# Seven-product form for the second block's values and late tile pairs, with work moved to GpSimd and ScalarE

## The chip, the cores and the metric

The kernel runs on one core of a Trainium2 chip. The metric is the device time of one execution in microseconds (us). Engines are named as the profile names them: PE is TensorE, PEld its weight loads, DVE VectorE, ACT ScalarE, POOL GpSimd, SP SyncE (which only issues DMAs here). All data is float32; TensorE runs one float32 matrix product as two records in the trace, so a count of records is twice the count of `matmul` calls.

## The reference, cut to what matters

The program is two blocks of a language model. The change is in the second block, which runs twice (DEPTH = 2) on 256 tokens of width 1024:

```python
def token_mixer(x, w_in, ...):
    m = x @ w_in                                   # 1024 -> 3*1024 + 2*1024 + 2*1024 columns
    q, k, v, xr, gr, gates = jnp.split(m, cuts, axis=-1)
    ya = diff_attention(q, k, v, lambda_qk, subln_g, lam_init)   # 8 heads, softmax twice per head
    h = rg_lru(causal_conv(xr, conv_w, conv_b), ...)             # 4 taps along the tokens
    yr = h * jax.nn.gelu(gr)
    g = jax.nn.sigmoid(gates.reshape(B, S, N_BRANCH, D_MODEL))
    merged = g[:, :, 0] * (ya @ w_br_attn) + g[:, :, 1] * (yr @ w_br_lru)
    return merged @ w_out

def causal_conv(xb, w, b):
    y = b + xp[:, 0:S] * w[0]
    for tap in range(1, CONV_W):
        y = y + xp[:, tap:tap + S] * w[tap]
```

Behind the mixer come a layer norm, a mixture of experts picked by key (`peer`) and a second layer norm.

## The kernel before, in words

The kernel is a chain of phases. Within a phase each engine has its own list of instructions in a fixed, hand-written order, and waits on semaphores; between phases all engines meet, so a phase ends when its last engine is done. Three phases in a row matter here, once in each of the two layers.

**Queries and keys, then values** (L2255 to L2452). `m = x @ w_in` is computed transposed, in tiles of 128 output columns by 256 tokens. Two such tiles (a tile pair, one 1 MB weight DMA) are one 2x2 block product, and eight pairs make the queries and keys. They are already in seven-product form (Strassen's scheme as Winograd arranged it): instead of eight products of half-size blocks, seven, with sums of weight blocks and of token blocks as operands. Each product is four calls of `product()` (L2296) of 128x128 by 128 columns, 28 calls for a pair. VectorE makes the four weight sums (`weight_sum`, L2353, 128x512 each) one pair ahead, and adds the partial results out of PSUM; ScalarE copies two parts. The seventh product, `onto` a PSUM bank, has to wait until VectorE has read that bank (semaphore `third`). The values follow as plain products: 32 calls of 128x128 by 512 columns (L2335), each of four PSUM banks copied out by VectorE (L2450).

**Attention with the late tile pairs** (L2454 to L2619). Attention is done in eight units (two heads by 128 query tokens). Units 0 to 3 see 128 keys ("early" here), units 4 to 7 see 256 ("late"). For each unit TensorE forms scores (L2503), VectorE adds the position bias and takes the maximum (L2559), ScalarE takes exponentials (L2602), VectorE sums them, scales and subtracts the two softmaxes (L2564 to L2571), TensorE turns the result (L2516) and multiplies it by the values (L2529), VectorE copies that out (L2578). The remaining 16 tile pairs of `x @ w_in`, the late pairs, are put between these steps on TensorE, two for each unit, as plain products: 16 calls of 128x128 by 256 columns for a pair (L2478), each result copied out of PSUM by one ScalarE instruction (L2588). VectorE does the convolution, one column tile in four instructions (L2547, L2549), in units 2 to 5. GpSimd does nothing. The last late product is split, and its second half is put behind the sums of squares over each head (`head_sums`, L253), whose root (L2616) and reciprocal (L2582) end the phase.

**Gates and branches** (from L2622), unchanged, begin with L2693 and L261 on TensorE; L261 reads the reciprocal.

SP's list of weight DMAs: `w.rest` alternates two buffers, so a load starts when the pair two before it is done.

Of the kernel before, what the change touches and what calls it, by code (L numbers as in the profile page):

```python
# [12 lines left out]
ALU = mybir.AluOpType  # L13
# [3 lines left out]
P = 128  # L17
D = 1024
# [2160 lines left out]
def second_block(nc, a, w, h, scaled, spare, cst, psum, psum_all):  # L2179

    with ExitStack() as ctx:
# [37 lines left out]
        for l in range(DEPTH):  # L2219
            tile = {n: (lambda i, n=n: a[n][l, i]) for n in ("w_in2", "br_attn", "br_lru", "w_out2", "peer_q")}  # L2220
            with ExitStack() as mixer:
# [14 lines left out]
                with ExitStack():  # L2236
# [8 lines left out]
                    part = arena[:, beside:beside + 4 * 2 * HALF].rearrange("p (q b t) -> p q b t", q=4, b=2)  # L2245
                    P1, P5, U2, U3 = range(4)
# [5 lines left out]
                    with phase(nc, "extra", "products", "weight_sums", "input_sums", "copied", "second", "third", "fourth", "taken", "scaled_out", "vectors", "v_weights", "v_ready", "soft_exp", "soft_log", "lam_sums", "lam_exp",  # L2252
                               "constants", "root", "h_ready", shared=w.landed[0]) as (block, S):
                        @block.sync
                        def _(sp):  # L2255
# [5 lines left out]
                            w.first(sp, 1, late_tile, W2)  # L2261

                        @block.scalar
                        def _(act):
# [3 lines left out]
                            for p in range(QK):  # L2268
# [8 lines left out]
                                if p % 2 == 0:  # L2277
                                    act.dma_start(wv[:, p:p + 2, :], a["w_v2"][l][:, p:p + 2, :]).then_inc(S.v_weights, 16)
# [9 lines left out]
                            act.activation(lam[:, 2:4], lam[:, 0:2], ACT.Exp).then_inc(S.lam_exp, 1)  # L2288
                            act.wait_ge(S.constants, 16)

                        @block.tensor
                        def _(pe):
# [35 lines left out]
                            pe.wait_ge(S.taken, 3 * QK)  # L2328
                            pe.wait_ge(S.v_weights, 16 * KD // 2)
                            if l == 0:  # L2330
                                pe.wait_ge(S.h_ready, KD)
                            for n in range(QT):
                                for half in range(2):
# [3 lines left out]
                                    mm.then_inc(S.v_ready, 1)  # L2337

                        @block.vector
                        def _(dve):  # L2340
# [13 lines left out]

                            def input_sum(n):
# [3 lines left out]
                                one, two = ((x_in[:, :, 0, hi], x_in[:, :, 0, lo]), (x_in[:, :, 1, hi], tin[:, 0]),  # L2359
# [35 lines left out]
                            for n in range(4):  # L2395
                                weight_sum(0, n)
                                input_sum(n)
# [1111 lines left out]
```

## Time and profile before

| | us |
|---|---|
| median of 3 runs (3458.3 to 3463.97) | 3458.74 |
| profiled execution | 3461.76 |
| its span | 3460.0 |
| PE busy in the span | 3157.5 |
| DVE busy | 2265.3 |
| ACT busy | 724.6 |
| POOL busy | 602.4 |
| queries and keys, layer 0, PE starts | 1493.5 |
| values, layer 0, PE starts | 1546.74 |
| attention phase, layer 0, PE starts | 1575.74 |
| next phase, layer 0, PE starts | 1707.58 |
| the same attention phase in layer 1, to the next phase | 2688.20 |

How to read it: PE is busy 91% of the span, and in the phases above nearly all the time; busy counts overlapping records once. The phases are read from a timeline, in which a row is a run of like instructions on one engine. "idle before" in brackets says how long the engine had nothing to do ahead of the row, and what ended that. Layer 1 repeats layer 0 within a few tenths of a microsecond, so every price below is read in layer 0 and counted twice.

### The profile page before, as it was taken

To read this page: it belongs to the slowest core of one execution; us is meant where nothing else is said; L and a number is where in the kernel's file an instruction comes from. 1 tells how busy PE (TensorE), PEld (TensorE's weight loads), DVE (VectorE), ACT (ScalarE), POOL (GpSimd) and SP (SyncE) were. 2 spreads that over 40 slices of the span, in tenths; PEclk is the share of its full clock that TensorE was granted. 3 is DMA by queue.
4 is the path that set the end of the run, shared out by engine and by line. 5 is a ranking of instruction groups with operands and counts; after the bars stand their busy time and mean duration, and the time that the engine had idled before them with its cause. 6 is when DMAs were issued, how large, how long until landed. Compare 5 with 4: busy or idle time off the path is not lost. (4 is left out here: it accounts for less than half of the span.)

```text
span 3460.0 us, 55458 instructions
## 1 busy us (share of the span) xinstructions
PE 3157.5 (91%) x20794; PEld 2381.9 (69%) x20794; DVE 2265.3 (65%) x5751; ACT 724.6 (21%) x1787; POOL 602.4 (17%) x520
## 2 busy tenths in 40 slices
PE   8999889999899999999998888888899989888877
PEld 8996679999878979987885444333678864434433
DVE  8844658778675558763458777776634567777775
ACT  2101311111131211111412222222212322222222
POOL 0000100000000000000004544445000035444442
PEclk9999899999999999999999999999999999999999
DMA  5443024444312024452449999999734479999998
GB/s 203 162 161 121 1 86 159 162 176 176 125 71 77 4 79 167 170 198 98 158 189 394 421 422 422 422 422 421 297 113 158 195 293 421 421 422 422 422 421 332
DMA packets 116014, 829.18 MB, mean 240 GB/s; under 512 B 12784, under 2 KB 14320, under 8 KB 17424
## 3 DMA queue, kind: packets, MB, share of 16 engines
q0 software_dynamic: 73728, 536.90, 37.4%
q1 hardware_dynamic: 39488, 273.59, 21.1%
q10 hardware_dynamic: 2576, 15.59, 1.3%
q8 instruction: 155, 2.54, 0.3%
q14 instruction: 67, 0.55, 0.0%
HBM read 824.99 MB, written 1.05 MB: 239 GB/s over the span
## 5 line engine op out<-in xcount | busy, mean ns | idle before, releaser
L3215 PE MATMUL psum_all<-expert_rows,const_sb 128*128 128x512 f32 x2048 | 971.3, 632 | 181.0 <-ACT const_sb L3130 180.1
L2803 POOL DMA_INDIRECT expert_rows<-in_peer_uv_dram,head_experts x512 | 593.1, 1158 | 2426.8 <-issue 1864.8
L3215 PEld LDWEIGHTS psum_all<-expert_rows,const_sb 128*128 128x128 f32 x2048 | 403.9, 202 | 730.6 <-issue 472.8
L2955 DVE CUSTOM_DVE_ANT_0 expert_rows<-expert_rows,xn 128x1024 f32<-128x1024 f32 x512 | 616.5, 1223 | 255.6 <-DMA expert_rows<-in_peer_uv_dram,head_experts 251.6
L2478 PE MATMUL psum_all<-x,weight_ring 128*128 128x256 f32 x1024 | 228.6, 381 | 0.0
L3130 ACT ACTIVATE const_sb<-cst,head_weights 128x128 f32<-128x128 f32 x496 | 158.6, 390 | 329.2 <-DVE head_weights L2966 318.4
L2478 PEld LDWEIGHTS psum_all<-x,weight_ring 128*128 128x128 f32 x1024 | 191.7, 190 | 28.8 <-issue 3.5
L409 PE MATMUL psum_all<-xn,weight_ring 128*128 128x136 f32 (+1 forms) x1408 | 193.0, 280 | 20.2 <-PEq L174 9.1
L409 PEld LDWEIGHTS psum_all<-xn,weight_ring 128*128 128x128 f32 x1408 | 176.6, 192 | 21.7 <-issue 9.8
L409 PE MATMUL psum_all<-xn,weight_sums 128*128 128x136 f32 (+1 forms) x1056 | 142.6, 278 | 0.7 <-DVEq L641 0.6
L3126 ACT ACTIVATE dots<-dots 128x4 f32<-128x4 f32 x124 | 25.5, 205 | 559.7 <-DVE dots L2955 559.7
L409 PE MATMUL psum_all<-input_sums,weight_sums 128*128 128x136 f32 (+1 forms) x1056 | 132.6, 278 | 0.1
L409 PEld LDWEIGHTS psum_all<-xn,weight_sums 128*128 128x128 f32 x1056 | 130.9, 191 | 1.2 <-issue 1.2
L409 PEld LDWEIGHTS psum_all<-input_sums,weight_sums 128*128 128x128 f32 x1056 | 126.8, 191 | 0.6 <-issue 0.4
L518 ACT ACTIVATE gate<-gate 128x272 f32<-128x272 f32 (+1 forms) x88 | 37.5, 426 | 361.2 <-DVE gate L611 361.2
L571 DVE TENSOR_TENSOR weight_sums<-weight_ring 128x512 f32<-128x512 f32 (+1 forms) x102 | 68.4, 671 | 58.7 <-PE psum_all L409 55.6
L409 PE MATMUL psum_all<-hidden,weight_ring 128*128 128x136 f32 (+1 forms) x704 | 88.7, 278 | 0.0
L3197 PE MATMUL psum_all<-x,weight_ring 128*128 128x256 f32 x384 | 84.8, 379 | 0.0
L409 PEld LDWEIGHTS psum_all<-hidden,weight_ring 128*128 128x128 f32 x704 | 84.4, 190 | 0.0
L3197 PEld LDWEIGHTS psum_all<-x,weight_ring 128*128 128x128 f32 x384 | 73.0, 190 | 15.0 <-issue 5.7
L2578 DVE COPY expert_rows<-psum_all 128x256 f32<-128x256 f32 x16 | 6.8, 424 | 114.5 <-PE psum_all L2529 114.5
L280 PE MATMUL psum_all<-xn,weight_ring 128*128 128x272 f32 x320 | 75.2, 398 | 0.0
(621 smaller groups left out, 5082.1 us busy)
## 6 DMA issues: line engine op xcount, KB each, us to landing
weight_ring<-in_ffn_in_dram SPq DMA_DIRECT2D x88, 1024.0 KB, 4.8
weight_ring<-in_w_in_dram SPq DMA_DIRECT2D x48, 1024.0 KB, 4.8
weight_ring<-in_ffn_out_dram SPq DMA_DIRECT2D x32, 1024.0 KB, 4.8
weight_ring<-in_ffn_out_dram SPq DMA_DIRECT2D x16, 768.0 KB, 4.2
weight_ring<-in_hyb_in_dram SPq DMA_DIRECT2D x12, 1024.0 KB, 4.8
weight_ring<-in_peer_q_dram SPq DMA_DIRECT2D x12, 1024.0 KB
expert_rows<-in_w_v_dram ACTq DMA_DIRECT2D x8, 1024.0 KB, 5.7
weight_ring<-in_br_attn_dram SPq DMA_DIRECT2D x8, 1024.0 KB, 6.8
```

What stands on the lines that cost most here:

```text
L280: mm = pe.matmul(banks[s * halves + h], wt[:, h, k, :], rhs[:, k, :], start=(k == 0), stop=(k == ktiles - 1))
L409: mm = pe.matmul(out, left(j), right(j), start=first and j == js[0], stop=end and j == js[-1], skip_group_check=onto)
L518: act.activation(gate[:, p % 2, :], gate[:, p % 2, :], ACT.Silu).then_inc(S.gate_ready, 1)
L571: dve.tensor_tensor(ws[:, 0], wt[:, 1, :, 0, :], wt[:, 1, :, 1, :], ALU.add).then_inc(S.weight_sums, 1)
L2478: mm = pe.matmul(late_bank(t)[:, half * T2:(half + 1) * T2], wt[:, half, k, :], h[:, k, :], start=(k == 0), stop=(k == KD - 1))
L2578: dve.tensor_copy(oa[:, 2 * hp:2 * hp + 2, n * P:(n + 1) * P], psum[5][:, 0:2 * P].rearrange("p (j t) -> p j t", j=2)).then_inc(S.attn_rea ...
L2803: pool.indirect_dma_start(out=rows[:, j, :], out_offset=None, in_=a["peer_uv"], in_offset=bass.IndirectOffsetOnAxis(ap=idx[:, n, j:j + 1], ...
L2955: dve.tensor_tensor_reduce(row, row, xt[:, n, :], 1.0, 0.0, ALU.mult, ALU.add, dots[:, n, j:j + 1]).then_inc(S.dotted, 1)
L3126: act.activation(dots[:, n, at], dots[:, n, at], ACT.Gelu_apprx_tanh).then_inc(S.gelus, 1)
L3130: act.activation(diag[:, j, :], ident, ACT.Copy, scale=wts[:, n, j:j + 1]).then_inc(S.diagonals, 1)
L3197: mm = pe.matmul(query_bank[:, c, :], wt[:, c, k, :], h[:, k, :], start=(k == 0), stop=(k == KD - 1))
L3215: mm = pe.matmul(sums(n, half), diag[:, j, :], rows[:, j, D + half * 512:D + (half + 1) * 512], start=False, stop=last and j == TOPK - 1)
```

## The change

1. The values take the seven-product form too: 7 products of 4 calls of 128x128 by 512 columns (28 calls in place of 32). VectorE makes their weight sums (`v_sum`, eight instructions of 128x1024) and, in layer 0, new token sums (`v_input`), in the last pair of the keys and beside the values' own products. Their weights are requested in the first four tile pairs instead of every second one.
2. The 16 late pairs take the seven-product form with 128 columns: 28 calls of `product()` in place of 16 with 256 columns. They use one set of four PSUM banks; the scores now have one buffer in place of two.
3. The four weight sums of each late pair are made by GpSimd (128x512 each), those of the first two pairs already at the end of the values' phase. They wait until the pair two before has been multiplied.
4. Results of a late pair leave PSUM by three ScalarE copies and four VectorE additions, with a fifth addition between two SBUF tiles, all 128x128.
5. The convolution leaves VectorE: ScalarE forms four products of 128x256 for a column tile (`conv_products`), after the pairs named in `CONV_AFTER`, and GpSimd adds three of them (`add_tap`), two additions after each pair's sums from pair 5 on.
6. Scores of the next unit are added on VectorE, and their exponentials taken on ScalarE, within the present unit.
7. Weight loads of the late pairs use three buffers.

In the rows of order below, `psum_all` is PSUM, `weight_ring` the raw weights as they land, `expert_rows` the big SBUF tile that holds everything else of this phase, `x` the tokens. TensorE in the fifth unit (unit 4, 256 keys) stood so before:

```order
L2503 MATMUL psum_all<-expert_rows 128x256 x4
L2478 MATMUL psum_all<-x,weight_ring 128x256 x16
L2516 MATMUL psum_all<-cst,expert_rows 128x128 x4
L2478 MATMUL psum_all<-x,weight_ring 128x256 x16
L2529 MATMUL psum_all<-expert_rows 128x128 x4
```

The same place of the changed kernel, as far as the transposes (L2692):

```order
L2675 MATMUL psum_all<-expert_rows 128x256 x4
L2623 MATMUL psum_all<-x,weight_ring 128x128 x4
L2623 MATMUL psum_all<-expert_rows 128x128 x12
L2623 MATMUL psum_all<-x,weight_ring 128x128 x4
L2623 MATMUL psum_all<-x,expert_rows 128x128 x4
L2623 MATMUL psum_all<-expert_rows,weight_ring 128x128 x4
L2692 MATMUL psum_all<-cst,expert_rows 128x128 x4
```

The 16 calls have become seven products of four; the last of them is the seventh product, which waits for `third`. A second pair of the same rows follows the transposes.

VectorE in that unit stood so before, from the copy of the unit ahead (L2578) on, the convolution at its end:

```order
L2578 COPY expert_rows<-psum_all 128x2x128
L2559 ISA expert_rows<-psum_all,const_sb 128x256
L2562 TENSOR_SCALAR expert_rows<-expert_rows 128x4
L2564 TENSOR_REDUCE expert_rows<-expert_rows 128x4
L2565 RECIPROCAL expert_rows<-expert_rows 128x4
L2566 TENSOR_SCALAR expert_rows<-expert_rows,lam 128x2
L2568 TENSOR_SCALAR expert_rows<-expert_rows 128x256 x2
L2571 SCALAR_TENSOR_TENSOR expert_rows<-expert_rows 128x256 x2
L2547 TENSOR_SCALAR expert_rows<-expert_rows,vec_sb 128x256
L2549 SCALAR_TENSOR_TENSOR expert_rows<-expert_rows,vec_sb 128x256 x3
```

and stands so in the changed kernel, where L2721 and L2724 are the two additions that release `second` and `third`:

```order
L2772 COPY expert_rows<-psum_all 128x2x128
L2757 TENSOR_REDUCE expert_rows<-expert_rows 128x4
L2758 RECIPROCAL expert_rows<-expert_rows 128x4
L2759 TENSOR_SCALAR expert_rows<-expert_rows,lam 128x2
L2761 TENSOR_SCALAR expert_rows<-expert_rows 128x256 x2
L2764 SCALAR_TENSOR_TENSOR expert_rows<-expert_rows 128x256 x2
L2721 TENSOR_TENSOR expert_rows<-expert_rows,psum_all 128x128
L2724 TENSOR_TENSOR expert_rows<-expert_rows,psum_all 128x128
L2747 ISA expert_rows<-psum_all,const_sb 128x256
L2750 TENSOR_SCALAR expert_rows<-expert_rows 128x4
L2731 TENSOR_TENSOR expert_rows<-expert_rows,psum_all 128x128
L2734 TENSOR_TENSOR expert_rows<-expert_rows 128x128
```

The softmax of the unit now stands directly ahead of `third`, and the bias and maximum of the next unit (L2747, L2750) behind it.

At the end of the phase TensorE had eight calls of the last late pair behind `head_sums` (L253):

```order
L2529 MATMUL psum_all<-expert_rows 128x128 x4
L2478 MATMUL psum_all<-x,weight_ring 128x256 x4
L253 MATMUL psum_all<-expert_rows,cst 8x256 x8
L2478 MATMUL psum_all<-x,weight_ring 128x256 x8
```

and has four half as wide now:

```order
L2704 MATMUL psum_all<-expert_rows 128x128 x4
L2623 MATMUL psum_all<-x,weight_ring 128x128 x4
L2623 MATMUL psum_all<-x,expert_rows 128x128 x4
L253 MATMUL psum_all<-expert_rows,cst 8x256 x8
L2623 MATMUL psum_all<-expert_rows,weight_ring 128x128 x4
```

The diff, cut to its core:

```diff
+ v_product(v_bank[0], lambda j: h_pairs[:, j, 0, lo], lambda j: v_raw[:, j, 0, :, 0, :])
+ pe.wait_ge(S.v_sums, 2)
+ v_product(v_bank[1], lambda j: tin[:, 0, j, :], lambda j: v_sums[:, 0, j])
...
+ pe.wait_ge(S.v_third, 1)
+ v_product(v_bank[3], lambda j: tin[:, 3, j, :], lambda j: v_raw[:, j, 1, :, 1, :], onto=True)
- for k in range(KD):
-     mm = pe.matmul(psum[4 + 2 * n + half][:, :], h[:, k, n * P:(n + 1) * P], wv[:, k, half * 512:(half + 1) * 512],
-                    start=(k == 0), stop=(k == KD - 1))
+ @block.gpsimd                       # phase of the values
+     pool.wait_ge(S.products, PRODUCTS * QK)
+     pool.wait_ge(S.v_products, 4)
+     pool.wait_ge(S.v_sums, 8)
+     for t in range(2):              # the four weight sums of late pairs 0 and 1
...
+ @block.gpsimd                       # phase of the attention
+     def add_tap(n):
+         k = n // 3
+         pool.wait_ge(S.tap_products, n + k + 2)
+         if n % 3:
+             pool.wait_ge(S.taps_added, n)
+         pool.tensor_tensor(xc[:, k, :], xc[:, k, :], tap_product(n), ALU.add).then_inc(S.taps_added, 1)
+     for t in range(EARLY_SUMS, LATE):
+         pool.wait_ge(*late_landed(S, t))
+         pool.wait_ge(S.products, PRODUCTS * (t - 1))
+         pool.tensor_tensor(ws[:, 0], wt[:, 1, :, 0, :], wt[:, 1, :, 1, :], ALU.add).then_inc(S.weight_sums, 1)
+         pool.wait_ge(S.weight_sums, done + 1)
+         pool.tensor_tensor(ws[:, 1], ws[:, 0], wt[:, 0, :, 0, :], ALU.subtract).then_inc(S.weight_sums, 1)
+         pool.tensor_tensor(ws[:, 2], wt[:, 0, :, 0, :], wt[:, 1, :, 0, :], ALU.subtract).then_inc(S.weight_sums, 1)
+         pool.wait_ge(S.weight_sums, done + 2)
+         pool.tensor_tensor(ws[:, 3], wt[:, 0, :, 1, :], ws[:, 1], ALU.subtract).then_inc(S.weight_sums, 1)
+         if t >= 5:
+             add_tap(2 * t - 10)
+             add_tap(2 * t - 9)
+ CONV_AFTER = {2: 0, 4: 1, 5: 2, 7: 3, 8: 4, 10: 5, 11: 6, 13: 7}
  @block.tensor
  for u, (hp, n) in enumerate(units):
-     if u + 1 < len(units):
+     if 0 < u and u + 1 < len(units):
          score(u + 1)
-     late_product(per_unit * u)
+     late_begin(2 * u)               # products 1 to 4
+     late_onto(2 * u)                # 5 and 6: wait for ScalarE's two copies
+     late_end(2 * u)                 # 7: waits for third
      pe.wait_ge(S.probs, u + 1)
...
+ @block.vector
+     for u in range(len(units)):
+         if u:
+             late_take(2 * u - 1)
+             take_out(u - 1)
+         weigh(u)
+         late_parts(2 * u)           # second, third
+         if u + 1 < len(units):
+             add(u + 1)
+         late_take(2 * u)
+         late_parts(2 * u + 1)
+ @block.scalar
+     for u, (hp, n) in enumerate(units):
+         copy_parts(2 * u)
+         if u:
+             head_squares(u - 1)
+         take_low(2 * u)
+         if u + 1 < len(units):
+             exps(u + 1)
+         conv_products(2 * u)
+         act.wait_ge(S.turned, u + 1)
...
+         copy_parts(2 * u + 1)
```

## Rows read from the trace of the kernel before

**Rows 1.** Windows, keys and attention: us, then PE, PEld, DVE, ACT, POOL busy, clock.
```profile
1493.00:1546.70 53.70, 52.25 (x449) 51.73 (x448) 43.29 (x101) 10.46 (x24) 0.00 (x0) 0.97 0.67 249
1575.70:1707.50 131.80, 130.66 (x664) 111.39 (x664) 51.37 (x170) 28.86 (x66) 0.00 (x0) 1.00 0.38 136
```

**Rows 2.** Groups: the late products in the attention phase; busy, mean ns, idle.
```profile
L2478 PE MATMUL psum_all<-x,weight_ring 128*128 128x256 f32 x512 | 114.3, 381 | 0.0
```

**Rows 3.** Timeline: last key pair, then the values; start, length, engine, line.
```profile
1540.73 2.76 PEld L2296 LDWEIGHTS psum_all<-expert_rows 128*128 128x128 f32 x24
1543.41 0.97 PEld L2296 LDWEIGHTS psum_all<-xn,weight_ring 128*128 128x128 f32 x8
1546.74 27.73 PE L2335 MATMUL psum_all<-expert_rows,x 128*128 128x512 f32 x64 [0.38 <-DVE expert_rows L2386]
```

**Rows 4.** Timeline of PE: unit 1 begins, unit 2 begins, then unit 4 to unit 5.
```profile
1591.58 0.72 PE L2503 MATMUL psum_all<-expert_rows 64*128 64x128 f32 x8
...
1606.91 0.72 PE L2503 MATMUL psum_all<-expert_rows 64*128 64x128 f32 x8
...
1654.40 1.14 PE L2503 MATMUL psum_all<-expert_rows 64*128 64x256 f32 x8
...
1655.47 7.17 PE L2478 MATMUL psum_all<-x,weight_ring 128*128 128x256 f32 x32
...
1669.83 1.05 PE L2529 MATMUL psum_all<-expert_rows 128*128 128x128 f32 x8
...
1670.81 1.14 PE L2503 MATMUL psum_all<-expert_rows 64*128 64x256 f32 x8
```

**Rows 5.** Timeline of DVE and ACT within a unit of 256 keys.
```profile
1656.97 1.71 ACT L2602 ACTIVATE expert_rows<-expert_rows 128x256 f32<-128x256 f32 x4 [2.76 <-DVE expert_rows L2562]
1658.71 1.22 DVE L2564 TENSOR_REDUCE expert_rows<-expert_rows 128x4 f32<-128x1024 f32 x1 [1.77 <-ACT expert_rows L2602]
...
1661.10 0.88 DVE L2571 SCALAR_TENSOR_TENSOR expert_rows<-expert_rows 128x256 f32<-128x256 f32 x2
...
1670.99 0.42 DVE L2578 COPY expert_rows<-psum_all 128x256 f32<-128x256 f32 x1 [5.11 <-PE psum_all L2529]
```

**Rows 6.** Timeline in the first block: all places where POOL computes beside DVE.
```profile
384.12 2.89 POOL L1211 TENSOR_TENSOR qd<-gq,eg 128x1280 f32<-128x1280 f32 x1 [48.92 <-ACT eg L1251]
384.25 0.42 DVE L1130 CUSTOM_DVE_ANT_0 fox_s<-psum_all,weight_ring 16x272 f32<-16x272 f32 x1
...
385.07 1.96 DVE L1134 TENSOR_SCALAR fox_stat<-fox_stat 16x2 f32<-16x2 f32 x1
...
389.28 0.71 DVE L1194 TENSOR_TENSOR fox_s<-fox_s,fox_stat 16x544 f32<-16x544 f32 x1
...
392.81 2.89 POOL L1215 TENSOR_TENSOR kbg<-kb,eg 128x1280 f32<-128x1280 f32 x1
...
393.60 2.68 DVE L1194 TENSOR_TENSOR fox_s<-fox_s,fox_stat 16x544 f32<-16x544 f32 x1
```

**Rows 7.** Timeline: end of the attention phase and first product of the next.
```profile
1699.36 3.62 PE L253 MATMUL psum_all<-expert_rows,cst 128*8 128x256 f32 x16
...
1702.91 3.72 PE L2478 MATMUL psum_all<-x,weight_ring 128*128 128x256 f32 x16
1703.02 0.37 ACT L2616 ACTIVATE rs<-psum_all 8x256 f32<-8x256 f32 x1 [3.10 <-PE psum_all L253]
1703.49 1.74 DVE L2582 RECIPROCAL rs<-rs 8x256 f32<-8x256 f32 x1 [5.26 <-ACT rs L2616]
...
1707.58 1.97 PE L2693 MATMUL psum_all<-expert_rows 128*128 128x256 f32 x8 [0.94 <-PEq L174]
```

**Rows 8.** Groups: the instructions whose like are added; busy, mean ns, idle.
```profile
L2353 DVE TENSOR_TENSOR expert_rows<-weight_ring 128x512 f32<-128x512 f32 x16 | 11.0, 685 | 2.1 <-PEq L174 2.1
L2367 DVE TENSOR_TENSOR expert_rows<-expert_rows,psum_all 128x128 f32<-128x128 f32 x8 | 2.3, 282 | 2.0 <-PE psum_all L2296 2.0
L2594 ACT ACTIVATE expert_rows<-expert_rows 128x256 f32<-128x256 f32 x8 | 3.2, 403 | 2.5 <-DVE expert_rows L2578 2.5
```

More of the change, by code:

```diff
@@ L2251, in second_block @@
                     quad = lambda p: [psum[4 * (p % 2) + i][:, 0:HALF] for i in range(4)]
-                    with phase(nc, "extra", "products", "weight_sums", "input_sums", "copied", "second", "third", "fourth", "taken", "scaled_out", "vectors", "v_weights", "v_ready", "soft_exp", "soft_log", "lam_sums", "lam_exp",
-                               "constants", "root", "h_ready", shared=w.landed[0]) as (block, S):
+                    QUARTER = D // 4
+                    v_sums = arena[:, NQK * (PADC + T2):NQK * (PADC + T2) + 4 * KP * 2 * QUARTER].rearrange("p (s j g m) -> p s j g m", s=4, j=KP, g=2)
@@ L2327, in _, with v_product @@
                                 product(bank[3], lambda j: wt[:, 1, j, 1, :], lambda j: tin[:, 3, j, :], onto=True)
-                            pe.wait_ge(S.taken, 3 * QK)
-                            pe.wait_ge(S.v_weights, 16 * KD // 2)
+                            def v_product(out, left, right, onto=False):
+                                for j in range(KP):
+                                    mm = pe.matmul(out, left(j), right(j), start=j == 0 and not onto, stop=j == KP - 1, skip_group_check=onto)
+                                mm.then_inc(S.v_products, 1)
@@ L2459, in second_block @@
                     pt = area(work + 8 * T2, 2, QT, P)
[L2460 to L2466 removed]
+                    st = area(work + 8 * T2 + 2 * QT * P, 2, 4, 4)
@@ new lines, in second_block @@
+                    late_quad = [psum[b][:, 0:HALF] for b in (6, 7, 2, 3)]
+                    late_out = lambda t: (z[:, NQK + 2 * t, PADC:], z[:, NQK + 2 * t + 1, PADC:])
+                    with phase(nc, "extra", "products", "weight_sums", "copied", "second", "third", "fourth", "taken", "low_taken", "scores", "added", "shifted", "exps", "probs",
+                               "turned", "turned_in", "attn_out", "attn_read", "o_squares", "o_sums", "o_root", "tap_products", "taps_added", shared=w.landed[1]) as (block, S):
@@ L2552, in _, with late_parts @@
-                            for u, (hp, n) in enumerate(units):
+                            def late_parts(t):
+                                bank, b = late_quad, t % 2
+                                dve.wait_ge(S.products, PRODUCTS * t + 3)
+                                dve.wait_ge(S.copied, 2 * t + 1)
+                                dve.tensor_tensor(part[:, U2, b, :], part[:, P1, b, :], bank[2], ALU.add).then_inc(S.second, 1)
+                                dve.wait_ge(S.products, PRODUCTS * t + 4)
+                                dve.wait_ge(S.second, t + 1)
+                                dve.tensor_tensor(part[:, U3, b, :], part[:, U2, b, :], bank[3], ALU.add).then_inc(S.third, 1)
@@ L2553, in _, with add @@
+                            def add(u):
+                                hp, n = units[u]
                                 kn = (n + 1) * P
@@ L2590, in head_squares, with exps @@
+                            def exps(u):
+                                act.wait_ge(S.shifted, u + 1)
+                                for c in range(4):
+                                    s = s_sb[:, u % 2, c, 0:(units[u][1] + 1) * P]
+                                    last = act.activation(s, s, ACT.Exp, bias=st[:, u % 2, 3, c:c + 1], scale=AD ** -0.5)
+                                last.then_inc(S.exps, 1)
                             def head_squares(u):
```

300 lines of the change are left out of this document (224 added, 76 removed).

## The prediction

> **What bounds the kernel now.** I read the page first (PE busy 91%), then the windows of the three phases, then the timeline of single units. In the keys PE is busy 52.25 of 53.70 us, in the attention phase 130.66 of 131.80, while DVE works 51.37, ACT 28.86 and POOL not at all [rows 1]. So TensorE's own work is the length of these phases, and a product taken away is worth its full time, as long as nothing that feeds TensorE comes late. The reader is to see in the timeline of PE that its rows follow each other without a gap [rows 4].
>
> **What the change takes away.** A late pair costs 114.3 / 16 = 7.14 us [rows 2]. In the seven-product form a pair is 56 records; 24 of them take 1543.41 - 1540.73 = 2.68 us in the keys, which run this form now, so 0.112 us each and 6.25 us a pair [rows 3]. Gain 0.89 x 16 = 14.2 us a layer. The values are 27.73 us for 32 calls; 28 of the same shape are 24.3, gain 3.5 us, and the 0.38 us that PE waits ahead of them goes too, since the new banks are free sooner [rows 3]. Against it, VectorE has four value sums twice as long as a weight sum (0.685 us, [rows 8]) ahead of the last key pair's additions: that pair's seventh product comes about 0.3 us late. Values: 3.5 a layer. The other value sums and token sums end on VectorE about 7 us after the keys, under products 1 and 2 (3.5 us each) or later; product 6 needs the last sums, which are made during product 4. The eight early GpSimd sums start at the end of product 4, and three products, 10.4 us, stand beside them; at 1.2 us each (below) they end at 10, just inside. Request times of the weights move by a few us in queues with room; I cost that at nothing. If nothing waited, two layers would give 2 x (14.2 + 3.5) = 35.4 us.
>
> **What it adds, and where it lies on the path.** GpSimd: a 128x1280 addition-like instruction takes 2.89 us [rows 6]; in proportion 128x512 takes 1.16. The trace has no such row. Below I bound it by this 1.16; above by 2.89 itself, since a fixed part can't be excluded from one size. I take 1.2, near the proportional end, which is where the one row points. A pair's four sums are then 5.1 us with the steps between, two additions of the convolution 1.4: 6.5 against 7 to 8 us for a pair and its share of attention. GpSimd keeps up, and has 6 us of lead before TensorE would wait for a sum.
>
> But GpSimd holds VectorE up. While POOL computes from 384.12 to 387.01, a DVE TENSOR_SCALAR of 16x2 lasts 1.96 us and ends at 387.03; the second L1194, begun at 393.60, takes 2.68 us where the first took 0.71, and ends 0.58 after POOL does at 395.70. The CUSTOM instruction that reads PSUM and one SBUF tile, in between, takes its usual 0.42 [rows 6]. I carry that over: in the attention phase every TENSOR_SCALAR and every instruction with two SBUF inputs waits for the running POOL instruction; reductions and additions out of PSUM don't. The Trainium skill, "SBUF — State Buffer", Who interferes with whom, says the same more sharply: one port pair is shared, held for a whole instruction, and the second to issue blocks fully; the trace agrees in its three overlaps. By that rule alone the sum is the one made here.
>
> Now one late unit, time 0 where the unit's scores begin. TensorE: scores 1.07 [rows 4], six products of 0.89, so the seventh could start at 6.4. VectorE: sees the end of the product with the values at 0.2, copies 0.4, the chain from reduction to subtraction 3.27 (1658.71 to 1661.98, [rows 5]), two additions of 0.28 [rows 8] with 0.2 between and behind: `third` at 4.6. Spare: 1.8 us. GpSimd starts its sums when the pair ahead ends, 1 us before 0 (1669.83 to 1670.81, [rows 4]), so it runs 1.2 us instructions from -0.9 to 4.2 and convolution additions to 5.7. In the 3.27 us chain the first TENSOR_SCALAR comes at 2.0 and waits to 2.95 (0.9); the scaling pair behind it finds the next POOL instruction begun, 1.1; the subtraction pair finds an addition of the convolution, 0.55. Together 2.55, less the spare 1.8: the seventh product waits 0.8 us. Of a pair of like instructions I let only the first wait; if each does, 0.6 more. In an early unit the chain is shorter by 0.8 and the scores by 0.5, and the same three waits leave 0.7. The last unit has no scores ahead of it, so 0.8 + 1.07 = 1.85. Over the eight units: 0.2 + 0.7 + 0.75 + 0.2 + 3 x 0.8 + 1.85 = 6.1 us a layer (in unit 3 the scores are already long and the chain still short).
>
> Behind `third` stands the next unit's bias and maximum, then its small TENSOR_SCALAR at 8.7, again behind a POOL instruction (begun at 8.2): 9.4. ScalarE waits for it, then exponentials 1.71 to 11.3 [rows 5], and, after pairs 2, 4, 8 and 10, four products of the convolution at 0.4 [rows 8] to 13.0; then the copy of the turned result 0.6 and of the first part of the odd pair 0.3: 13.9. TensorE has the odd pair's first four products done at 12.1 and stands until 14.0: 1.9 us in units 4 and 5. Without convolution ScalarE is in time, but VectorE frees the bank of the odd pair's second product about 0.5 late (units 3 and 6, together 1.15); early units 0.15 twice. Sum 5.25 us a layer.
>
> The end: `head_sums` runs 1699.36 to 1702.91, then 3.55 us of products cover root and reciprocal (to 1705.23) [rows 7]. Now 0.89 covers them. DVE's last addition waits for that product and ends 1.4 after `head_sums`, the reciprocal 1.74 later, the meeting of engines 0.3: next phase at 3.5 to 3.7 in place of 4.67. Of the 2.7 that TensorE saves here 1.7 isn't had.
>
> **Sum.** A layer: 14.2 - 6.1 - 5.25 - 1.7 + 3.5 = 4.7; two layers 9.4 us. The profiled execution took 3461.76, the span 3460.0; 3461.76 - 9.4 = 3452.4. The median of the runs shown is 3.0 lower, so 3449.
>
> **Rivals.** (a) *The waits are light.* If VectorE's held instructions slip between POOL's, or an own start falls past a boundary, 1.3 us of waits in place of 2.55 stays within the spare 1.8. Left are the end, 1.7, and about 1.5 a layer for ScalarE and the last unit: gain 2 x (14.2 + 3.5 - 3.2) = 29, time 3430. For it: the waits sit just above a threshold. Against: sums and chain both start from TensorE's steps, so their order is the same in each unit. (b) *Each held instruction waits*, 0.6 more in six units, 3.6 a layer: 9.4 - 7.2 = 2.2, time 3456.5. (c) *Slower: GpSimd's 128x512 costs more than proportion.* Each 0.1 us adds 0.3 in seven chains and 0.1 in the stretch behind, 2.8 a layer, 5.6 in all. No gain is left at 1.2 + 0.17 = 1.37 us; at 1.6 us four sums and two additions take 8.4 us, more than a pair, TensorE also waits for sums, and the loss is 22 - 9 = 13 or more: 3472. From 1.48 us on it is slower by over 7 us. A fixed part of 0.5 us in each POOL instruction would do; at the upper bound, 2.89, 56 sums alone need 162 us in a phase of 118, and the time would be near 3550. The Trainium skill, "GPSIMD Engine Reference", Elementwise — side-by-side cycle accounting, gives 4497 ns for 2048 columns; with the 2.89 us row a line through both would give 1.3 us, an estimate, and by it 3455. (d) *The change does as it says without any hold*: 35.4 less the end 3.4 and 1 of ScalarE, 31: 3428. The low end.
>
> **How the numbers follow.** Forecast as walked, 3443 to 3453, 0.42. Light waits or none (a, d), 3428 to 3443: 0.27. More waits (b, or c up to 1.45 us), 3453 to 3465: 0.19. Slower (c beyond): 0.12. About 0.2%, 7 us, is what can be told from no change. Faster (below 3451.8): 0.27 and 0.34 of the 0.42, together 0.61. Same: the other 0.08 and 0.19, together 0.27. Slower: 0.12. The range takes the low end of (d) and stops a little below the slow case: 3429 to 3464.
>
> **What would show it.** The values' 56 records in 24.3 us; a late pair on PE 6.25 where nothing waits; POOL TENSOR_TENSOR of 128x512 at 1.2 us; in the chain of each unit, DVE TENSOR_SCALAR and SCALAR_TENSOR_TENSOR of 1 us or more that end with a POOL instruction; PE idle 0.7 to 0.9 us ahead of the seventh product of even pairs, released by the VectorE addition L2724; 1.9 us in units 4 and 5, released by ScalarE's copy; the next phase 3.6 us behind `head_sums`. Wrong if the held instructions keep their old length, if POOL's means lie above 1.4 us, or if PE waits for weight sums.

## The result and the profile after

| | before | after |
|---|---|---|
| median, us | 3462.29 (3458.3 to 3466.28, 11 runs) | 3467.48 (3462.78 to 3475.72, 11 runs) |
| ratio, 95% interval | | 1.0022 [1.0014, 1.003] |
| span of the profiled execution | 3460.0 | 3464.1 |

The change makes the kernel slower by about 0.2%. The prediction said 3449 in a range of 3429 to 3464: wrong in sign and outside the range.

Starts of the phases on TensorE give the length of each phase, in us:

| | before, layer 0 / 1 | after, layer 0 / 1 |
|---|---|---|
| queries and keys | 53.25 / 53.43 | 52.23 / 53.05 |
| values | 29.00 / 29.00 | 25.54 / 25.53 |
| attention with late pairs | 131.84 / 131.82 | 134.48 / 134.46 |
| gates, up to the first branch product | 11.21 / 11.22 | 19.47 / 19.47 |
| from there to the next layer's keys, or to the end | 755.2 / 760.6 | 750.3 / 756.8 |

Windows of the kernel after, the phases of layer 0 and last the gates of layer 1; columns as in [rows 1] (us, then PE, PEld, DVE, ACT, POOL busy, granted clock):

```profile
1492.76:1544.99 52.23, 51.46 (x448) 51.10 (x449) 46.41 (x101) 9.97 (x24) 0.00 (x0) 0.98 0.69 252
1544.99:1570.53 25.54, 24.21 (x59) 10.49 (x57) 15.02 (x37) 2.23 (x5) 10.25 (x8) 1.00 0.08 33
1570.53:1705.01 134.48, 123.55 (x1049) 115.99 (x1049) 86.11 (x218) 44.48 (x131) 87.78 (x80) 1.00 0.38 134
1705.01:1724.48 19.47, 19.47 (x49) 13.93 (x50) 5.83 (x11) 10.02 (x22) 0.00 (x0) 0.56 0.41 162
2687.82:2707.29 19.47, 19.47 (x49) 13.90 (x50) 5.83 (x11) 10.06 (x22) 0.00 (x0) 0.56 0.42 162
```

The window of the gates in the kernel before:

```profile
1707.58:1718.79 11.21, 11.21 (x48) 8.79 (x49) 5.53 (x11) 8.84 (x21) 0.00 (x0) 1.00 0.71 283
```

Two things are to be seen. In the attention phase PE is busy 7.1 us less than in [rows 1], but idle 10.9 us in place of 1.1. And in the gates, whose instructions the change doesn't touch, the same work takes 8.26 us more: PE is busy all the time, and its granted clock is 0.56 in place of 1.00.

PE's timeline at that place, which answers to [rows 7] (start, length, line, records, idle before):

```profile
1697.60 3.62 PE L253 MATMUL psum_all<-expert_rows,cst 128*8 128x256 f32 x16
1701.15 1.16 PE L2623 MATMUL psum_all<-expert_rows,weight_ring 128*128 128x128 f32 x8
...
1705.01 2.64 PE L2939 MATMUL psum_all<-expert_rows 128*128 128x256 f32 x8 [2.70 <-PEq L174]
1707.58 3.78 PE L261 MATMUL psum_all<-rs,cst 8*128 8x256 f32 x8
1711.29 3.78 PE L2939 MATMUL psum_all<-expert_rows 128*128 128x256 f32 x8
...
1718.71 5.93 PE L2939 MATMUL psum_all<-expert_rows 128*128 128x256 f32 x16
```

The idle ahead of the gates has grown from 0.94 to 2.70 us. Behind it eight records of L2939 soon take 3.78 us where they took 1.97 in [rows 7]: TensorE runs at the lower of its two levels, 1.2 GHz in place of 2.4, until late in the last row.

What PE waited for from the attention phase to the meeting behind it (who waited, for whom; us in total, times, longest):

```profile
PE psum_all L2623 <- DVE expert_rows L2724: 4.5, 5, 2.2
PE psum_all L2939 <- PEq L174: 2.7, 1, 2.7
PE psum_all L2623 <- DVE expert_rows L2731: 2.0, 4, 0.7
PE psum_all L2623 <- ACT expert_rows L2799: 1.7, 2, 0.9
```

L2724 is the addition `third`, L2731 the one that frees the bank of the second product, L2799 ScalarE's copy of the first product. The unit that the prediction walked, unit 4, from where its scores begin (1629.79):

```profile
1632.13 1.27 POOL L2607 TENSOR_TENSOR expert_rows<-weight_ring 128x512 f32<-128x512 f32 x1
1632.23 2.60 DVE L2761 TENSOR_SCALAR expert_rows<-expert_rows 128x256 f32<-128x256 f32 x2
1633.36 1.32 POOL L2609 TENSOR_TENSOR expert_rows<-weight_ring,expert_rows 128x512 f32<-128x512 f32 x1
1634.65 1.64 POOL L2597 TENSOR_TENSOR expert_rows<-expert_rows 128x256 f32<-128x256 f32 x2
1634.87 1.70 DVE L2764 SCALAR_TENSOR_TENSOR expert_rows<-expert_rows 128x256 f32<-128x256 f32 x2
1636.49 0.27 DVE L2721 TENSOR_TENSOR expert_rows<-expert_rows,psum_all 128x128 f32<-128x128 f32 x1
1636.87 0.29 DVE L2724 TENSOR_TENSOR expert_rows<-expert_rows,psum_all 128x128 f32<-128x128 f32 x1
1637.21 1.16 PE L2623 MATMUL psum_all<-expert_rows,weight_ring 128*128 128x128 f32 x8 [0.73 <-DVE expert_rows L2724]
```

The two instructions of the scaling pair L2761, asked for one by one, run from 1632.23 to 1633.55 and from 1633.48 to 1634.83: each ends 0.15 us behind a POOL instruction (1633.40 and 1634.68). The pair takes 2.60 us in place of some 0.7. `third` ends at 1637.16, and the seventh product waits 0.73 us for it.

### The profile page after: what moved, and what is told of

Its sections match the earlier page's. It is cut to its first block and busy times, and to the rows that moved or that the text cites. A ratio compares the mean times of both kernels' runs of the same rounds, so it can differ in the third digit from the quotient of the medians.

```text
span 3464.1 us, 57647 instructions
## 1 busy us (share of the span) xinstructions
PE 3133.3 (90%) x21546; PEld 2388.9 (69%) x21546; DVE 2356.7 (68%) x5869; ACT 760.7 (22%) x1921; POOL 793.0 (23%) x696
## 5 line engine op out<-in xcount | busy, mean ns | idle before, releaser
L3461 PE MATMUL psum_all<-expert_rows,const_sb 128*128 128x512 f32 x2048 | 956.0, 624 | 193.5 <-ACT const_sb L3376 193.4
L2623 PE MATMUL psum_all<-expert_rows 128*128 128x128 f32 x768 | 91.6, 276 | 4.0 <-DVE expert_rows L2731 4.0
L2623 PEld LDWEIGHTS psum_all<-expert_rows 128*128 128x128 f32 x768 | 88.3, 192 | 5.3 <-POOL expert_rows L2604 5.3
L3443 PE MATMUL psum_all<-x,weight_ring 128*128 128x256 f32 x384 | 84.8, 379 | 0.0
L3443 PEld LDWEIGHTS psum_all<-x,weight_ring 128*128 128x128 f32 x384 | 73.0, 190 | 15.0 <-issue 5.7
```

The source lines that it names most:

```text
L2623: mm = pe.matmul(out, left(j), right(j), start=j == 0 and not onto, stop=j == KP - 1, skip_group_check=onto)
L3443: mm = pe.matmul(query_bank[:, c, :], wt[:, c, k, :], h[:, k, :], start=(k == 0), stop=(k == KD - 1))
L3461: mm = pe.matmul(sums(n, half), diag[:, j, :], rows[:, j, D + half * 512:D + (half + 1) * 512], start=False, stop=last and j == TOPK - 1)
```

## Experiments

All ratios are to the kernel before, run beside each. Lengths of stretches and stops are those of the profiled execution. Edits are cut to their core, and are against the kernel after unless said otherwise. "Theory C" in some expectations is the reading above: the idle at the meeting lets TensorE's clock fall.

**1. Cover for the idle.** Five matmuls whose result nobody reads, behind the last product of the phase:

```diff
+ for j in range(5):
+     pe.matmul(banks[0], ident, h[:, j, :], start=True, stop=True)
```

> The changed kernel with five more 128x128 by 256-column products behind the attention phase's last late product, into a PSUM bank that nobody reads (2.2 us of work, in the 2.70 us that PE stands idle there). Theory C (the idle stretch lets PE's granted clock fall, and the next phase then runs at half speed for 19.5 us): the phase's length stays 134.5 us a layer, PE's granted clock in the 19.5 us behind it is 1.0 again instead of 0.56, and that stretch shrinks from 19.5 to about 11.2 us; the kernel gets 16 us faster than the changed one, about 3451, 0.3% under the kernel before. Rival (the slow stretch comes from its inputs or from other engines): stretch and time unchanged, about 3467.

Measured: 3463.77, ratio 1.0006 [0.9996, 1.0016]. Layer 0:

```profile
1690.30 1.66 PE L2623 MATMUL psum_all<-expert_rows,weight_ring 128*128 128x128 f32 x8 [2.22 <-DVE expert_rows L2726]
...
1707.13 1.96 PE L2941 MATMUL psum_all<-expert_rows 128*128 128x256 f32 x8 [0.54 <-PEq L174]
1709.02 1.99 PE L261 MATMUL psum_all<-rs,cst 8*128 8x256 f32 x8
```

With 0.54 us of idle the gates take 11.21 us in both layers, as before. The meeting is the same, at the same 3.86 us behind the sums over the heads, only filled: without the idle the gates weren't slow. The gain in time was a third of what was expected, 0.16% or some 5.5 us between the ratios of the two kernels. In layer 0 the clock now fell for a moment inside the last unit (1.66 where eight such records take 1.16), 1.7 us in the phase, and the stretch from the branches to the next layer took 755.2 us, not the 750.3 of after (761.4 and 756.8 in layer 1).

**2. GpSimd made thin.** The sums and additions of GpSimd in the attention phase on one column (so the late pairs' and convolution's values are not computed); all waits stay:

```diff
- pool.tensor_tensor(ws[:, 0], wt[:, 1, :, 0, :], wt[:, 1, :, 1, :], ALU.add)
+ pool.tensor_tensor(ws[:, 0, 0, 0:1], wt[:, 1, 0, 0, 0:1], wt[:, 1, 0, 1, 0:1], ALU.add)
```

> The changed kernel with GpSimd's weight sums and additions in the attention phase cut to one column each (the rest of them is left out), all waits kept. Theory W (VectorE's held instructions wait for running GpSimd instructions): no TENSOR_SCALAR or SCALAR_TENSOR_TENSOR of more than 0.9 us, no PE wait for the addition that releases the seventh product except 0.7 in the last unit, the phase 134.5 - 7 = about 127.5 us a layer; the slow stretch behind it stays. Time about 3467 - 14 = 3453. Rival (the units are long because of ScalarE and the order of steps, not GpSimd): phase 133 or more, time above 3463.

Measured: 3444.41, 0.9937 [0.9921, 0.9953]. The attention phase is 123.00 us in both layers, and no stop behind L2724, L2731 or L2799 is left. The groups of DVE, of after and then of this kernel (line, shape, count, busy us, mean ns):

```profile
L2761 DVE TENSOR_SCALAR expert_rows<-expert_rows 128x256 f32<-128x256 f32 x8 | 8.8, 1134 | 0.1
L2759 DVE TENSOR_SCALAR expert_rows<-expert_rows,lam 128x2 f32<-128x2 f32 x8 | 7.8, 973 | 0.3
L2764 DVE SCALAR_TENSOR_TENSOR expert_rows<-expert_rows 128x256 f32<-128x256 f32 x8 | 6.1, 803 | 0.1
```

```profile
L2764 DVE SCALAR_TENSOR_TENSOR expert_rows<-expert_rows 128x256 f32<-128x256 f32 x8 | 3.5, 482 | 0.1
L2761 DVE TENSOR_SCALAR expert_rows<-expert_rows 128x256 f32<-128x256 f32 x8 | 2.5, 351 | 0.1
L2759 DVE TENSOR_SCALAR expert_rows<-expert_rows,lam 128x2 f32<-128x2 f32 x8 | 1.8, 228 | 0.3
```

An instruction on two elements a partition takes 973 ns beside GpSimd and 228 without. The whole price of letting GpSimd's 80 instructions do their work is 134.48 - 123.00 = 11.5 us a layer. The idle at the meeting was still 2.69 us. Behind it the clock was low for some 4 us in layer 0 (gates 12.85), and for longer in layer 1 (20.72, which is 9.5 over 11.21).

**3. The values alone** (against before: only the values in seven-product form, the late pairs as they were):

> The kernel before with the values alone in seven-product form: late pairs, convolution and attention as before, nothing on GpSimd. Theory: values' phase 3.4 us shorter in each layer, attention 131.8 us and the next phase 11.2 us as before; time 7 us under the kernel before (ratio 0.998). Rival (the values' part costs elsewhere, for instance by its earlier weight requests in the keys): ratio 1.000 or more.

Measured: 3456.14, 0.9979 [0.997, 0.9988], values 25.53 us, attention phase 131.82, gates 11.22. That half of the change brings what was predicted of it.

**4. The idle alone, in the kernel before.** The whole last late product is done ahead of the sums over the heads, so nothing covers root and reciprocal:

```diff
+ late_part(last_late, 1, range(KD)).then_inc(S.late_ready, 1)
  head_sums(...)
- late_part(last_late, 1, range(KD)).then_inc(S.late_ready, 1)
```

> The kernel before, with the half late product that stands behind the sums over heads put ahead of them, so that PE has nothing while root and reciprocal are made: PE idle there 0.94 + about 3.0 = 3.5 to 4 us, no other change. Theory C: phase 3 us longer a layer, and PE's granted clock falls behind it: the first 11.2 us of the next phase become 19 us. Time +6 +16 = about 22 us over the kernel before. Rival (the clock falls for another reason, for instance the shape of the products before it): +6 us only.

Measured: 3478.28, 1.0041 [1.0028, 1.0055]. Layer 0, then layer 1:

```profile
1711.49 1.97 PE L2693 MATMUL psum_all<-expert_rows 128*128 128x256 f32 x8 [2.79 <-PEq L174]
...
2692.65 2.75 PE L2693 MATMUL psum_all<-expert_rows 128*128 128x256 f32 x8 [2.79 <-PEq L174]
2695.33 3.78 PE L261 MATMUL psum_all<-rs,cst 8*128 8x256 f32 x8
```

An idle of 2.79 us, without GpSimd and without seven products, let the clock fall in layer 1 (gates 19.46) and not in layer 0 (11.22). So the idle can do it alone, but doesn't do it each time. The phase grew by 1.6 us a layer, not by the 3 that was expected.

**5. Softmax steps first.** VectorE does the next unit's `weigh` behind `late_parts(2 * u + 1)`, ahead of the additions at the unit's end, so `third` has no softmax ahead of it:

```diff
- weigh(u)                     # at the start of unit u
+ weigh(u + 1)                 # at the end of unit u, and weigh(0) ahead of the loop
```

> VectorE does the softmax steps of the next unit (weigh) ahead of the copies and additions that serve the present one, so they no longer stand between a unit's scores and the addition `third`. After shows five stops of TensorE behind that addition in a layer, 4.5 us of idle, and with each stop about 0.27 us more is lost (the row ahead drains, the first row behind fills: 0.16 and 0.11). Theory A (the stops are VectorE's softmax chain, stretched by GpSimd): the five stops go, 5.8 us a layer, 11.7 in all; the stops behind the bank copies (2.0) and ScalarE (1.7) stay, and so does the idle of 2.70 us with the low clock behind it. With after at 3468 beside this kernel before at 3463: 3456. Theory B (VectorE is simply too busy beside GpSimd, wherever the steps stand): the time reappears as stops behind the copies of the banks, 3465 or more.

Measured: 3448.87, 0.9967 [0.9956, 0.9978]. The attention phase fell from 134.48 to 128.65 us: 5.83, where 5.8 was expected. All five stops behind `third` went, ScalarE's two went with them, and five stops behind the bank addition L2731 stand there (0.64, 1.14, 0.48, 0.44, 1.75: 4.5 us in place of 2.0). So theory B has a part, and that the sum came out at 5.8 is partly luck: ScalarE's two stops, expected to stay, gave about as much as the stops behind the bank took. In the profiled execution the rest of the gain came from the gates, which weren't slow this time, with the idle before them unchanged:

```profile
1700.73 1.97 PE L2941 MATMUL psum_all<-expert_rows 128*128 128x256 f32 x8 [2.70 <-PEq L174]
```

**6. The convolution after other pairs.**

```diff
- CONV_AFTER = {2: 0, 4: 1, 5: 2, 7: 3, 8: 4, 10: 5, 11: 6, 13: 7}
+ CONV_AFTER = {2: 0, 3: 1, 5: 2, 7: 3, 9: 4, 11: 5, 13: 6, 14: 7}
```

> The convolution's products on ScalarE (and the additions on GpSimd behind them) follow pairs 2, 3, 5, 7, 9, 11, 13 and 14 in place of 2, 4, 5, 7, 8, 10, 11 and 13, so in units 4 and 5 ScalarE copies the turned result and the first part of the odd pair without four products of 0.4 us ahead. Theory A: the two stops of 0.87 us behind ScalarE's copy go, with their drain and fill 2.3 us a layer: 3463.5 where after stands at 3468. Theory B (they wait for the exponentials, which VectorE lets go late, and the products cost nothing): unchanged, 3468. Shown by the idle ahead of the products released by ScalarE in units 4 and 5.

Measured: 3464.98, 1.0015 [1.0005, 1.0025]. Both stops behind ScalarE are gone, and attention is 132.51 in layer 0: theory A, less 0.2 us for a last stop of 2.45 in place of 2.22. In layer 1 it is 134.05, since 1.6 us went behind that last stop: the granted clock from there to the sums over the heads is 0.82, where layer 0 has 1.00. The clock fell behind the idle of 2.70 in layer 0 (gates 19.47), and in layer 1 it didn't (11.21).

**7. Reciprocal first.** The whole `late_take` of the last pair moved behind the reciprocal:

```diff
- late_take(LATE - 1)
  dve.wait_ge(S.o_root, 1)
  step(dve.reciprocal(rs2[0:AH, :], rs2[0:AH, :]))
+ late_take(LATE - 1)
+ dve.wait_ge(S.taken, 2 * LATE)
```

> VectorE takes the reciprocal of the head sums ahead of the last pair's addition, and so the idle of TensorE at the meeting of the engines falls from 2.70 to about 1.7 us. Theory A (the idle lets TensorE's granted clock fall, and the shorter idle does not): 1 us of idle a layer and the slow stretch of 19.5 us gone, which gave 8.3 us in the gate's products, less what the expert stage had given back (4.9 and 3.8 us): 3458 where after stands at 3468. Theory B (any stop of this size lets it fall): 1 us a layer alone, 3466.

Measured: 3474.93, 1.0037 [1.0022, 1.0052]. Neither theory: the idle fell only to 2.41, since three additions that had stood ahead of the root now came behind it:

```profile
1711.45 1.74 DVE L2789 RECIPROCAL rs<-rs 8x256 f32<-8x256 f32 x1 [5.32 <-ACT rs L2864]
1713.22 0.29 DVE L2731 TENSOR_TENSOR expert_rows<-expert_rows,psum_all 128x128 f32<-128x128 f32 x1
1713.43 0.29 DVE L2734 TENSOR_TENSOR expert_rows<-expert_rows 128x128 f32<-128x128 f32 x1
1713.63 0.28 DVE L2736 TENSOR_TENSOR expert_rows<-expert_rows,psum_all 128x128 f32<-128x128 f32 x1
```

The clock fell in both layers (gates 19.46 and 19.47), and also behind the last unit's stop of 2.2 us (granted 0.82 from there to the sums), so the phase took 135.86 and 136.13 us in place of 134.48. The idle was too little changed, 2.41 beside 2.70, to say whether a shorter one protects.

**8. All together, with four matmuls as cover.**

> All three at once (softmax steps of the next unit first, the convolution after other pairs, the reciprocal first), and four matmuls 128x128x256 without use in front of the meeting, so that TensorE idles under 1 us there. By the stops read from the trace: 5.8 and 2.3 us a layer, the end 0.8, and the low clock gone, 8.3 a layer less the 4.9 and 3.8 us that the expert stage gave back. Theory A: 2 x (5.8 + 2.3 + 0.8) + 7.8 = 25.6 under after's 3468, so 3442, faster than this kernel before by 21 us. Theory B (GpSimd's hold moves on to the next step): the stops behind the bank copies grow to 1 us and more, and the time is 3452 or above.

Measured: 3444.95, 0.9951 [0.9938, 0.9964]. Idle at the meeting 0.69, gates 11.21 in both layers, attention 128.02. The five stops behind the bank addition stayed (0.65, 1.14, 0.49, 0.50, 1.34), so theory B has its part. The timeline says why: the addition L2733 stands in VectorE's queue behind the subtraction pair, which takes 2.78 us beside GpSimd (two of 482 ns in experiment 2).

```profile
1653.55 2.78 DVE L2766 SCALAR_TENSOR_TENSOR expert_rows<-expert_rows 128x256 f32<-128x256 f32 x2
...
1656.25 0.28 DVE L2733 TENSOR_TENSOR expert_rows<-expert_rows,psum_all 128x128 f32<-128x128 f32 x1
1656.67 2.92 PE L2623 MATMUL psum_all<-expert_rows 128*128 128x128 f32 x24 [0.49 <-DVE expert_rows L2733]
```

**9 and 10. The kernel after, and that of experiment 5, each once more.** No edit.

> The changed kernel, unaltered, in a second profiled execution. It asks whether the low granted clock behind the idle of 2.70 us belongs to the kernel or to the execution. Theory A (the kernel's pattern of stops decides it): again a slow stretch of 19.5 us at the gate in both layers, 3464. Theory B (an idle of this length lets the clock fall in some executions and not in others, since the same 2.70 us was followed by it in 7 of 12 layers so far): the same stops to 0.02 us, but a slow stretch in one layer or in none, or one of another length, and a time 4 us away for each layer that differs.

> The kernel with the next unit's softmax steps first, unaltered, in a second profiled execution. In its first the idle of 2.70 us stood in both layers without a slow stretch behind it. Theory A (its pattern of stops protects it): again none, attention phase 128.6 us, span 3443. Theory B (chance of the execution): a slow stretch at the gate in one layer or both, 8.3 us each on the spot, some 4 of it left at the end: 3447 or 3451.

Measured: 3471.71 and 3449.89 in one execution each. After: the same stops to 0.03 us, gates 19.47 in both layers, as expected by theory A; its span is still 5.9 us longer than in its first execution, 3.6 of it behind the gates of layer 1 (760.4 us for 756.8). The kernel with the softmax first: attention 128.63 and 128.65, but gates 12.86 in layer 0 (first row behind the idle below) and 11.21 in layer 1, where its first execution had 11.21 twice.

```profile
1703.27 3.21 PE L2941 MATMUL psum_all<-expert_rows 128*128 128x256 f32 x8 [2.70 <-PEq L174]
```

Neither theory is whole: the execution has a say, the kernel too.

**11. The bank addition inside the softmax.** Experiment 8, with VectorE's `late_take` in three parts: the one that frees the second product's bank goes between scaling and subtraction of `weigh`, and at the end only the very last addition stands behind the reciprocal:

```diff
  step(last)                   # in weigh(u + 1), behind the scaling pair
+ late_bank1(2 * u + 1)
  for j in range(2):
      last = dve.scalar_tensor_tensor(...)
```

> All changes of the last run together, and in VectorE's queue the addition that frees the second product's bank moved from behind the softmax steps of the next unit to between them, and the reciprocal at the end put ahead of only the very last addition. The run before showed five stops behind that addition, 0.65, 1.14, 0.49, 0.49 and 1.34 us in a layer, each with 0.27 us of drain and fill: 5.4 us a layer. Theory A (the order in the queue made these stops): they go, the attention phase falls from 128.0 to about 122.5 us, and the time is 3445 - 11 = 3434, 0.992 of the kernel before. Theory B (VectorE has no room left beside GpSimd): the stops come back behind another of its instructions, 3440 or more.

Measured: 3436.66 (3430.75 to 3444.31), 0.9932 [0.9916, 0.9948], some 23 us under the kernel before. Attention 125.08, gates 11.22, idle at the meeting 0.30. The five stops are gone; two others are left in a layer, behind the addition that frees the fourth product's bank (L2743):

```profile
1637.96 1.13 PE L2623 MATMUL psum_all<-expert_rows 128*128 128x128 f32 x8 [0.65 <-DVE expert_rows L2743]
1683.50 1.13 PE L2623 MATMUL psum_all<-expert_rows 128*128 128x128 f32 x8 [0.83 <-DVE expert_rows L2743]
```

The phase is 2.6 us longer than the 122.5 that theory A gave. Up to the sums over the heads it takes 118.34 us, only 2.75 more than with GpSimd made thin (115.59).

## Why the prediction was wrong

**The values: right.** 3.46 us a layer against 3.5; experiment 3 has them alone.

**GpSimd's durations and its hold on VectorE: right, but for pairs.** GpSimd's groups in the attention phase:

```profile
L2607 POOL TENSOR_TENSOR expert_rows<-weight_ring 128x512 f32<-128x512 f32 x14 | 18.0, 1286 | 0.0
L2597 POOL TENSOR_TENSOR expert_rows<-expert_rows 128x256 f32<-128x256 f32 x24 | 18.0, 756 | 1.3
```

128x512 takes 1.27 to 1.29 us (1.2 taken), 128x256 takes 0.76 (0.7 taken). Rival (c), which needed 1.48 to be slower, didn't happen; its price of 5.6 us for each 0.1 us would have made 4.5 us of the 0.08 more, and the stops came out only 0.15 us a layer longer. The estimate of 1.3 us by the figure in the Trainium skill, "GPSIMD Engine Reference", Elementwise — side-by-side cycle accounting, was nearer than the proportion. That GpSimd holds VectorE's TENSOR_SCALAR and its instructions with two SBUF inputs came true; that of a pair of like instructions only the first waits did not. In unit 4 each of the scaling pair waited, 1.9 us in place of the 1.1 walked, as rival (b) had it, while the small TENSOR_SCALAR ahead of it waited only 0.3 (0.51 us where it takes 0.23), not 0.9.

**The stops: right in sum, with some luck.** The walk had 6.1 behind `third` and 5.25 behind the chain to ScalarE and the banks, 11.35 us a layer. Experiment 2 puts them at 11.5. But the eleven stops seen are 8.2 us of idle; another 3.0 is the drain and fill at them, 0.27 each (0.16 and 0.11, read for experiment 5), which the walk didn't have. One by one: `third` in units 4, 5 and 6 0.73, 0.62 and 0.62 (0.8 predicted), in the last unit 2.22 (1.85), in unit 2 0.31 (0.75), and units 0, 1 and 3 show none (0.2, 0.7, 0.2). Units 4 and 5 behind it each show 0.45 and 0.87 of idle, with the drain and fill 1.9, as predicted, but a third of the idle stands behind the bank addition and not behind ScalarE. Experiments 2, 5 and 6 took GpSimd's work, the softmax ahead of `third` and the convolution ahead of ScalarE's copy away one at a time, and the stops behind each went. An instruction of two elements a partition took 973 ns beside GpSimd's and 228 without. The Trainium skill, "SBUF — State Buffer", Who interferes with whom, says that whoever issues first has the shared port pair for its whole instruction, and the other is blocked; that agrees.

**The gain of the late pairs: mis-sized, the first failed step.** "A late pair costs 114.3 / 16 = 7.14" [rows 2] adds lengths of rows, and a row is some 0.1 to 0.2 us longer than its distance to the next start, since its end overlaps with that. By starts, a unit's first pair took 7.01 us and its second 6.91: from 1655.47 [rows 4] to the transposes at 1662.48, and from 1662.92 to 1669.83 [rows 4].

```profile
1662.48 0.60 PE L2516 MATMUL psum_all<-cst,expert_rows 128*128 128x128 f32 x4
1662.92 7.07 PE L2478 MATMUL psum_all<-x,weight_ring 128*128 128x256 f32 x32
```

In seven products, where nothing waits, the same two pairs take 6.35 and 6.25 us; a unit of experiment 2:

```profile
1653.29 1.16 PE L2623 MATMUL psum_all<-x,weight_ring 128*128 128x128 f32 x8
...
1659.64 0.60 PE L2692 MATMUL psum_all<-cst,expert_rows 128*128 128x128 f32 x4
1660.08 1.06 PE L2623 MATMUL psum_all<-x,weight_ring 128*128 128x128 f32 x8
...
1666.33 1.06 PE L2704 MATMUL psum_all<-expert_rows 128*128 128x128 f32 x8
```

So one side of the difference was a sum of lengths and the other a distance of starts, taken where no scores stand ahead. The gain is 0.66 x 16 = 10.6 us a layer, not 14.2: 7.2 us too much over both layers.

**The end: right as far as it went, and there the second failed step.** The next phase came 3.86 us behind the sums over the heads (3.5 to 3.7 predicted), so of 2.66 us saved 1.85 wasn't had (1.7). But the step counted only the idle. It asked which engine is late next, and not what the stop does to TensorE's own clock: the cover of 3.55 us had kept the idle at 0.94, and behind 2.70 us the gates took 8.26 us more in the profiled execution. Experiment 1 filled the idle, and they took 11.21 again. No term, rival or bound had that; the prediction read the granted clock in [rows 1] as 1.00 and never asked what kept it there.

**The sum anew.** A layer: 10.6 for the pairs and 0.2 for a short stop of the kernel before that is gone (0.22, ahead of its last transposes at 1694.43), less 11.5 for the stops and 1.85 for the end, is -2.55; the phase shows -2.64. With 3.46 for the values it would be 0.8 us faster a layer; with 8.26 lost in the gates it is 7.4 us slower. So the wrong size of the pairs' gain alone took the 9.4 us forecast down to some 2, which can't be told from no change, and experiment 1, without slow gates in its profile, stands at 1.0006. In the profiled execution the first block and the keys took 2.1 us less in all, and what follows the gates 4.9 and 3.8 us less, so the two spans differ by 4.1. The interval of the ratio, 0.14 to 0.30%, is 5 to 10 us.

**What stays open.** Whether those 4.9 and 3.8 us are given back by the stretch behind, or chance: its length in layer 0 was 750.3 and 751.3 in the two executions of after, but 753.5 and 754.0 in the two others with slow gates there (experiments 7 and 6), 754.5 to 756.2 in seven with none or a short one, and 752.6 and 751.7 in experiments 8 and 11. In layer 1 the five executions with gates slow throughout have 756.8 and 760.4 (after, twice), 757.1, 760.2 and 760.7, and the eight others 758.1 to 761.9, so the 3.8 of layer 1 can well be chance. Experiment 1's profile, with 16.5 us less in the gates and 9.5 us more behind them, says that part of such a gain isn't kept in that execution. From 1900 to 2400 us the DMA engines move the experts' rows at 421 or 422 GB/s in each window of 100 us, in both kernels, so something else than TensorE may set the length there; that wasn't tried. How often the clock falls in the executions that weren't profiled isn't known either.

## What to carry to other kernels

Count a change of TensorE's work in distances between starts on both sides, never a sum of lengths against a distance. Before taking work that covers a wait, ask not only how long the idle gets, but what the granted clock is in the products behind it; a few matmuls without use cost nothing in a wait, and behind such a wait the gates took 11.21 us in place of 19.47, though of that only some 5.5 us in both layers came through to the time in experiment 1. Work moved to GpSimd stretched VectorE's TENSOR_SCALAR and its instructions with two SBUF inputs, down to one of two elements, so put ahead of them, in VectorE's queue, what TensorE waits for: that order took 5.8 us a layer off the phase in experiment 5 and 2.9 between experiments 8 and 11. With it, the cover and the later convolution, the change that lost 0.2% gains 0.7%. And if a held instruction has a like one behind it, count the wait for each of them.

## What the runs showed of the hardware

The fall of the clock has chance in it. Idles of 2.41 to 2.79 us stood ahead of the gates in 16 layers: the gates were slow throughout (19.46 to 20.72 us) in 9, slow for a short while (12.85 and 12.86) in 2, and at full clock in 5. Idles of 0.30 to 0.94 stood there in 10 layers, and none was slow. Where TensorE had stopped for 2.2 us or more some 13 us earlier, 7 of 8 were slow (after and experiments 6, 7 and 9), and without such a stop 2 of 8 throughout. The count is small, and that the earlier stop has a part in it is an argument, not a result. Behind that stop itself the clock fell for a short while in 4 of 10 layers (granted 0.82 in place of 1.00 up to the sums over the heads, 1.6 us more). The Trainium skill, "TensorE: Matmul & The Clock Gate", Part 1: The HAM clock gate, says that the hardware's watch over TensorE runs freely and doesn't start with the kernel, so the same kernel meets it differently from run to run; experiment 10, the same kernel with 11.21 and 12.86 us in its first layer, agrees. A fall cost 1.6 or 8.3 us where it happened, once 9.5. Whether the spread between executions of one kernel comes from it is not shown: after spreads over 13 us (3462.78 to 3475.72), but the kernel before, whose gates were at full clock in its profile, spreads over 12 (3458.72 to 3470.61 in the 24 executions beside experiments 1 to 4).
